# A decode attention and the output projection behind it as one phase, and a row norm moved into the MLP's first step

## The reference

```python
hn = rmsnorm(h, norm_attn[l])                   # h = x
q, k, v = split(hn @ w_qkv_a)                   # q, k rotated; 8 heads, 2 maps of 64
o = diff_attend(q, q_pos, k_all, v_all, k_pos, lam)   # softmax of map 0 - lam * softmax of map 1
o = rmsnorm(o, subln_a[i]) * (1.0 - lam_init)   # per head of 128 columns, lam_init = 0.2
h = h + o.reshape(b, t, A_V) @ w_o_a[i]         # the output projection, 1024 x 1024
h = h + sq_relu_mlp(rmsnorm(h, norm_mlp[l]), w_up[l], w_down[l])   # 1024 -> 4096 -> 1024
```

## Time and profile before

| | |
|---|---|
| median of 3 runs | 3811.17 us (3806.93 to 3812.57) |
| the profiled execution: its time, its span | 3813.02 us, 3811.3 us |
| TensorE busy | 3467.8 us (91%), mean granted clock 0.955 |
| VectorE, ScalarE, GpSimd busy | 1720.6, 1131.1 and 568.2 us (45%, 30%, 15%) |
| transfers | 325.21 MB, mean 85 GB/s |
| `fused_attention` | to 572 us |
| decode attention of layer A (`da`) | 572 to 809 us |
| output projection (`oa`) | 809 to 969 us |
| first MLP (`m0`) | from 969 us |

### The profile page before, as it was taken

How to read it: one execution, slowest core, us unless ns; L and a number is a source line. 1 busy time by engine, 2 the same in 40 slices (tenths; PEclk the granted TensorE clock), 3 DMA queues, 4 the chain that set the end, 5 groups by cost and what they waited for, 6 DMA issues and landing times. The chain is left out here.

```text
span 3811.3 us, 60654 instructions
## 1 busy us (share of the span) xinstructions
PE 3467.8 (91%) x23426; PEld 3048.8 (80%) x23426; DVE 1720.6 (45%) x2995; ACT 1131.1 (30%) x2287; POOL 568.2 (15%) x284
## 2 busy tenths in 40 slices
PE   6999997859799999998899888959969799999998
PEld 6999996748799999997787767746657699999997
DVE  4777764436344444445013266634423344444445
ACT  4444443433211122222013066633322222221112
POOL 3323200020111111110222000000010111111110
PEclk9999998979899999999799989979989899999999
DMA  3111119850211111110222243337751111111111
GB/s 112 54 54 53 46 27 349 330 172 28 72 33 44 44 44 44 38 39 2 82 90 72 62 95 82 67 90 264 276 202 38 61 44 41 36 44 44 44 44 50
DMA packets 263451, 325.21 MB, mean 85 GB/s; under 512 B 112945, under 2 KB 196049, under 8 KB 263313
## 3 DMA queue, kind: packets, MB, share of 16 engines
q1 hardware_dynamic: 248528, 288.85, 23.8%
q10 hardware_dynamic: 13648, 30.49, 2.2%
q0 software_dynamic: 1152, 4.19, 0.4%
HBM read 283.69 MB, written 39.79 MB: 85 GB/s over the span
## 5 line engine op out<-in xcount | busy, mean ns | idle before, releaser
L753 DVE TENSOR_TENSOR h_rows<-h_rows,m_dn 128x512 f32<-128x512 f32 x576 | 391.4, 686 | 325.4 <-PE m_dn L334 325.4
L332 PE MATMUL m_dn<-m_dn_hi,m_hid_hi 128*128 128x512 f32 x1152 | 449.4, 390 | 0.0
L333 PE MATMUL m_dn<-m_dn_lo,m_hid_hi 128*128 128x512 f32 x1152 | 448.4, 389 | 0.0
L334 PE MATMUL m_dn<-m_dn_hi,m_hid_lo 128*128 128x512 f32 x1152 | 448.2, 389 | 0.0
L737 DVE TENSOR_TENSOR m_relu<-m_relu 128x384 f32<-128x384 f32 x192 | 157.2, 819 | 516.6 <-ACT m_relu L718 516.6
L658 POOL TENSOR_TENSOR m_up_lo<-m_up_raw,m_up_hi 128x2048 fp32r<-128x2048 f32 x32 | 147.6, 4612 | 933.8 <-ACT m_up_hi L708 933.8
L332 PE MATMUL m_up<-c_xt_hi,m_up_hi 128*128 128x384 f32 x768 | 261.9, 341 | 16.6 <-POOL m_up_lo L658 16.6
L332 PE MATMUL m_up<-b_xt_hi,m_up_hi 128*128 128x384 f32 x768 | 261.9, 341 | 16.6 <-POOL m_up_lo L658 16.6
L334 PE MATMUL m_up<-c_xt_hi,m_up_lo 128*128 128x384 f32 x768 | 259.6, 338 | 0.0
L333 PE MATMUL m_up<-b_xt_lo,m_up_hi 128*128 128x384 f32 x768 | 259.6, 338 | 0.0
L333 PE MATMUL m_up<-c_xt_lo,m_up_hi 128*128 128x384 f32 x768 | 259.5, 338 | 0.0
(11 more groups left out here) (319 smaller groups left out, 7210.4 us busy)
## 6 DMA issues: line engine op xcount, KB each, us to landing
da_k_tiles<-in_cache_a_k SPq DMA_DIRECT2D x64, 512.0 KB, 5.9
da_v_tiles<-in_cache_a_v SPq DMA_DIRECT2D x64, 512.0 KB, 5.5
m_up_raw<-in_w_up SPq DMA_DIRECT2D x32, 1024.0 KB, 5.4
m_dn_raw<-in_w_down SPq DMA_DIRECT2D x32, 1024.0 KB, 4.9
db_k_tiles<-in_cache_b_k SPq DMA_DIRECT2D x64, 512.0 KB, 4.6
db_v_tiles<-in_cache_b_v SPq DMA_DIRECT2D x64, 512.0 KB, 4.2
fa_w_raw<-in_w_qkv_a SPq DMA_DIRECT2D x48, 256.0 KB, 3.6
kv_w_raw<-in_w_kvf SPq DMA_DIRECT2D x16, 512.0 KB, 3.7
```

The source lines that it names most:

```text
L332: pe.matmul(out, lh, rh, start=start, stop=False)
L333: pe.matmul(out, lh, rl, start=False, stop=False)
L334: return pe.matmul(out, ll, rh, start=False, stop=stop)
L753: dve.tensor_tensor(hc, hc, dns[n % 3][:], ALU.add).then_inc(s_de, 1)
```

## The change

- `start_phase` is gone. Its loads (identity, gain, the other constants, the lambda vectors) are issued from ACT's queue at the start of `fused_attention`, and lambda is worked out in turns 1 and 2 of its loop.
- In `fused_attention`, ACT scales the first two weight halves by the gain while rounding them, and DVE makes their low parts; GpSimd keeps the others. The sums of squares of rows 3 to 8 are spread over turns 1 to 3, and their root is taken in turn 4. After each output tile ACT also squares it and sums it (`output_squares`, 64 small instructions) into `o_rstd`.
- `decode_project` replaces `decode_attention` of layer A and `oa`. Its steps are numbered `n` over all streams (9 per stream). From step 14 on, prompt row tile `r` takes 9 steps: in the first (`t` = 5) its 8 transposes, in each of the other eight 6 matmuls of 128x512 of its projection. The loops over streams are unrolled. SP loads `w_o_a` (4 MB, in 8 parts) between key tiles 3 and 4 of the first stream; ACT and DVE split it in steps 0 to 7, with the gain and the 0.8 in it. GpSimd scales the row by `o_rstd` (`scale_rows`). SP loads a row and its residual per stream (`load_rows`), behind a wait for the transposes of the row before. The last row tile, which holds the streams' own output, is stored, loaded, squared, scaled, transposed and projected after everything else.
- There is one bank for the transposed probabilities where there were two.
- `mlp_phase` of layer A does the row norm of its input itself (`pre`, tiles `m_first_`, in the buffers of `m_next_`): rows 0 to 3 ahead of the weights on ACT and DVE, rows 4 to 8 after the up groups 0 to 3; TensorE transposes three rows ahead of each column group `g`.

```diff
+        PRE_ROWS, PRE_LAST = [[4, 5], [6], [7], [8], [], []], 3
...
-            def step(i, last=False):
-                pe.wait_ge(s_ul, i + 2)
+            def step(i, last=False, rows=False):
                 for g in range(RG):
+                    if rows:
+                        for r in range(3 * g, 3 * g + 3):
+                            pre.tensor(pe, r)
+                        pre.ready(pe, 3 * g + 2)
+                    if g == 0:
...
+                    if rows:
+                        for r in PRE_ROWS[n]:
+                            pre.scalar(act, r)
+                        if n == PRE_LAST:
+                            pre.high(act, RT - 1)
...
+            if pre:
+                for r in range(4):
+                    pre.scalar(act, r)
             up_high(0)
-            with act.Fori(0, STEPS - 1) as i:
+            if pre:
...
+            act.dma_start(core.const[:, 0:P], table[:, 0:P]).then_inc(s_id, 16)
+            act.dma_start(gcol[:], gain.rearrange("(k p) -> p k", p=P), allow_slow_non_contiguous=True).then_inc(s_gain, 16)
+            act.dma_start(core.const[:, P:], table[:, P:]).then_inc(s_cst, 16)
+            for x, v in enumerate(lams):
+                act.dma_start(lv[:, x, :], v.rearrange("a d -> (a d)").partition_broadcast(P)).then_inc(s_lam, 16)
             x_high(0)
+            act.wait_ge(s_gain, 16)
             for k in range(HK):
                 weight_high(0, k)
-            x_square(1)
+            x_square(0)
             x_high(1)
             for k in range(HK):
                 weight_high(1, k)
-            for i in range(SLOTS + 3):
...
+                if i == 4:
+                    row_root(1, 3, RT)
+                if i == 1:
+                    act.wait_ge(s_dot, 2)
+                    act.activation(ex[:], dots[:], ACT.Exp).then_inc(s_le, 1)
                 v_rows(i - 1)
                 if i + 2 < RT:
...
+            def output_squares(j):
+                s = step(j)
+                if s is None:
+                    return
+                p, t = place(j)
+                bank_read(act, units["o", j])
+                if s:
+                    act.wait_ge(s_oq, s)
+                act.activation(osq[:], ost[:, s % 2], ACT.Square,
+                               accum_out=core.o_rstd[:, t, p:p + 1]).then_inc(s_oq, 1)
...
+        STEPS, FIRST = CT + 1, 14
...
+        def columns_of(n):
+
+            r, x = divmod(n - FIRST, STEPS)
+            return r if n >= FIRST and x == 0 and r < RT - 1 else None
+
+        def products_of(n):
+
+            r, x = divmod(n - FIRST, STEPS)
+            return (r, x - 1) if n >= FIRST and x and r < RT - 1 else None
...
+            def load_rows(r):
+                if r:
+                    sp.wait_ge(s_kt, 2 * use["x", r - 1] + 2)
+                sp.dma_start(orow[:], o_rows[r * P:(r + 1) * P, :]).then_inc(s_or, 16)
+                sp.dma_start(core.h[:, r, :], rows_of(*residual, r)).then_inc(s_h[r], 16)
...
+            for k in range(KT):
+                sp.dma_start(wraw[:, k, :], w_o[k * P:(k + 1) * P, :]).then_inc(s_wd[k], 16)
+            sp.dma_start(vn[:], v_new).then_inc(s_vn, 16)
+            for t in range(KR, CT):
+                load_k(0, t)
+            load_rows(0)
+            for b in range(1, NB + 1):
+                for t in range(CT + 2):
+                    if b < NB and t < CT:
+                        load_k(b, t)
+                    if t >= 2:
+                        load_v(b - 1, t - 2)
+                    if b >= 2 and t == 1:
+                        store(b - 2)
+                    if t == 7 and b < RT - 1:
+                        load_rows(b)
+            store(NB - 1)
+            sp.wait_ge(s_st, 16 * NB)
+            load_rows(RT - 1)
+
...
+            def scale_rows(r):
+                pool.wait_ge(s_or, 16 * (r + 1))
+                pool.wait_ge(s_qb, 2 * min(r + 2, NB) + 1)
+                o = orow[:].rearrange("p (h e) -> p h e", e=P)
+                if r in (0, RT - 1):
+                    pool.wait_ge(s_rt, 2 if r else 1)
+                root = core.o_rstd[:, r, :] if r < RT - 1 else stat[:]
+                pool.tensor_tensor(o, o, root.unsqueeze(2).to_broadcast([P, KT, P]), ALU.mult).then_inc(s_os, 1)
...
+            def row_products(r, x):
+
+                c, k0 = divmod(2 * x, KT)
+                if x == 0:
+                    banks_free(use["x", r] + 1)
+                if k0 == 0 and 2 * r + c:
+                    pe.wait_ge(s_av, 2 * r + c)
+                for k in range(k0, k0 + 2):
+                    if r == 0 and c == 0:
+                        pe.wait_ge(s_wl, k + 1)
+                    w = [v[:, k, c * HALF:(c + 1) * HALF] for v in (whi, wlo)]
+                    ins = product(pe, acc[:], (xhi[:, k, :], xlo[:, k, :]), w, k == 0, k == KT - 1)
+                if k0 + 2 == KT:
+                    ins.then_inc(s_am, 1)
+
...
+            for n, t, bs, bv in stages():
+                if products_of(n) is not None:
+                    row_products(*products_of(n))
+                if bv is not None:
+                    for pair in PROBS[t]:
+                        probs(bv, pair)
+                if bs is not None and t + 1 < CT:
+                    keys(bs, t + 1)
+                if bs is not None and t == CT and bs + 1 < NB:
+                    keys(bs + 1, 0)
+                if columns_of(n) is not None:
+                    row_columns(columns_of(n))
+                if bs is not None:
+                    scores(bs, t)
+                if bv is not None:
+                    for v in VALUES[t]:
+                        values(bv, v)
...
+            row_columns(RT - 1)
+            for x in range(KT):
+                row_products(RT - 1, x)
...
-        decode_attention(nc, core, "da", False, q[SEQ:ROWS, :], kv["ak_s"], kv["av_s"], cak, cav, None, None, None, ao,
-                         residual=(xp, xs))
+        decode_project(nc, core, "da", q[SEQ:ROWS, :], kv["ak_s"], kv["av_s"], cak, cav, ao,
+                       a["w_o_a"].rearrange("n d e -> (n d) e"), a["subln_a"][0, :].rearrange("(p o) -> p o", o=1), (xp, xs))
         with ExitStack() as rows:
             core.normed_rows(rows, "b")
-            dense_phase(nc, core, "oa", "head", a["subln_a"][0, :], ao,
-                        [(a["w_o_a"].rearrange("n d e -> (n d) e"), c, "add", c) for c in (0, HALF)],
-                        following=a["norm_mlp"][0, :])
```

More of the change, by code:

```diff
@@ L133, in scope, with __init__ @@
     return sb, ps, sem
[L137 to L178, removed]
 class Norm:
-    def __init__(self, core, sb, ps, sem, tag, kind, gain, src=None, buffers=2):
+    def __init__(self, core, sb, ps, sem, tag, kind, gain, src=None, buffers=2, share=None):
         self.core, self.kind, self.gain_src, self.src = core, kind, gain, src
-        self.xn, self.buffers = sb(f"{tag}xn", [P, buffers, D]), buffers
+        self.xn, self.buffers = share.xn if share else sb(f"{tag}xn", [P, buffers, D]), buffers
         self.own_rows = kind in ("rms", "final")
@@ L204, in __init__ @@
         if kind != "final":
-            self.bank = [ps(f"{tag}nt{i}", [P, 4, P]) for i in range(2)]
+            self.bank = share.bank if share else [ps(f"{tag}nt{i}", [P, 4, P]) for i in range(2)]
         self.s_pre, self.s_root, self.s_gain, self.s_sq, self.s_rs, self.s_xn, self.s_tp, self.s_hi, self.s_lo = (
@@ L625, in mlp_phase @@
         nxt = Norm(core, sb, ps, sem, "next_", "final" if y_rows else "rms", following, y_rows)
+        pre = Norm(core, sb, ps, sem, "first_", "rms", first, share=nxt) if first is not None else None
         NF, RG = FC // P, 3
@@ L693, in step @@
                         nxt.tensor(pe, r - 2)
-            with pe.Fori(0, STEPS - 1) as i:
+            if pre:
+                step(0, rows=True)
+            with pe.Fori(1 if pre else 0, STEPS - 1) as i:
                 step(i)
@@ L748, in step @@
                     low(n)
+                    if rows:
+                        for r in PRE_ROWS[n]:
+                            pre.vector(dve, r)
+                        if n == PRE_LAST:
+                            pre.low(dve, RT - 1)
                 for n in range(ND):
@@ L755, in step @@
                         nxt.vector(dve, r - 1)
-            with dve.Fori(0, STEPS - 1) as i:
+            if pre:
+                for r in range(4):
+                    pre.vector(dve, r)
+                step(0, rows=True)
+            with dve.Fori(1 if pre else 0, STEPS - 1) as i:
                 step(i)
@@ L761, in _, with fused_attention @@
             nxt.low(dve, RT - 1)
-def fused_attention(nc, core, tag, x_rows, gain, w, k_out, v_out, q_sample, o_rows):
+def fused_attention(nc, core, tag, table, lams, x_rows, gain, w, k_out, v_out, q_sample, o_rows):
     with ExitStack() as ctx:
@@ L903, in _ @@
             pool.wait_ge(s_gain, 16)
-            for n in range(2 * PAIRS):
+            for n in range(2, 2 * PAIRS):
```

(19 more changed lines are left out.)

461 lines of the change are left out of this document (439 added, 22 removed).

## The result

The changed kernel takes 3830.75 us (median of 5 runs, 3826.79 to 3832.03), the kernel before 3811.17 us (5 runs beside it): ratio 1.0053, 95% interval 1.0039 to 1.0066. It is slower by 19.6 us, where 33 us less were forecast. The profiled execution took 3832.03 us.

A forecast was written before the change was run, and what follows sets the result against it. Decode needs transfers, projection needs TensorE, and they stand one behind the other. Head -20, merged phase -54, MLP +40.5 sum to -33.5 from 3813.0: 3779.5, less 1.9, 3778 us; own range 3760 to 3792, ends 3750 and 3803.

The forecast's parts named there:

- Steps 14 to 71, "with 37 us a stream": Merged decode and projection: 37 us a stream between bounds of 31 and 38.7, so 58 steps take 238 us.
- the prediction's own sign of being wrong: Merged streams: the prediction called itself wrong if a stream took under 34 or over 40 us.
- half of the gaps filled: Merged streams: half of the 0.37 us gaps per step counted as remaining in the 37 us a stream.
- The end of the phase: After the merged steps: value-only steps 21 us instead of 26, then the last row's chain, 31 us in the sum.
- The head, "-20": Program start: turn 2 of `fused_attention` at 27 us instead of 47.33, a gain of 20 us, bounds 13 and 23.
- The first stream, "+5": Steps 0 to 7, where ACT and DVE also split 4 MB of weights: 5 us more, bounds 0 to 8.
- The MLP's first step, "+40.5": Norm in the MLP: first product +9.6 us, two pauses +26.6, lower clock +4.3; bounds +31 to +47.
- Number 2: Merged streams: value tiles queue behind the rows, TensorE waits 10.3 us a stream, 3831 us; chance 8%.
- Number 3: No tellable change: value-tile wait of 6 to 8 us, or unfilled gaps with head -13 us; 3811 us; chance 10%.
- Number 1: Merged streams: the decode's gaps are not filled, a stream takes 40 us, 3797 us; chance 20%.
- Number 4: MLP's first step: norm of rows 4 to 8 hides, two pauses go, 31 us less, 3747 us; chance 7%.
- The range's high end: Whole kernel: 3803 us, for the decode's gaps left unfilled together with a poorer head.

The follow-up runs named there:

- e_store_late: Changed kernel with SyncE issuing the output store at loop position 6 of a stream, not 1: 3798.02 us, ratio 0.9963.
- e_both_late: Changed kernel with the store at loop position 6, not 1, and the projection rows' loads at 9, not 7: 3776.64 us, ratio 0.9912.
- e_norm_move: Kernel before, with only the MLP's row norm moved into the MLP's first step: 3830.97 us, ratio 1.0045.
- e_head_only: Kernel before, with only the changed kernel's program start: 3798.92 us, ratio 0.9960.

## Why the prediction was wrong

The sign was wrong, and one step made it so. Against the profiled execution, 3832.0 where the sum said 3779.5:

1. *Steps 14 to 71, "with 37 us a stream".* **This step failed.** It was 44.3 us a stream, over 40, the prediction's own sign of being wrong. The six streams between 611.02 and 877.75 took 266.7 us where the sum has 222: 44.7 more. The sum went through SyncE's queue for the rows and value tile 6, and priced that wait at 2 us, once a stream; it came once a stream, 2.1 us in the mean. It did not go through the queue for the store, which the change also puts there, ahead of key tile 2. That wait stood in the sum at nothing, and it was 3.7 us in the mean. Nor did it price the lower clock behind either wait. With these the store costs 5.2 us a stream (44.3 to 39.1), the rows 2.8 (44.3 to 41.5). The 37 was meant for the rows ahead of value tile 6 and a store that blocks nothing. That kernel is `e_store_late`, and it took 39.1: 2 us too low even so. With both moved a stream takes 36.1 us, where the sum without its 2 us for the value tile says 35. So its other parts (half of the gaps filled, no gap worse) hold to about 1 us; each by itself was not measured.
2. *The end of the phase.* Forecast 68 us from the transposes of row 6 (16 + 21 + 31, the first for the four steps up to step 71), measured 77.3; in `e_both_late` 71 (828.2 to 899.3). So 6 of the 9 us are the same queue, in the last stream. The sum's terms for the last row's store (2.5 us) and load (4) stood on no row; they landed in 1.9 and 3.3 us.
3. *The head, "-20".* Turn 2 began at 26.2 us (forecast 27), but turns 2 to 4 then took 7 us more than before, 5.1 of them in two waits for VectorE's `fa_qT`; a microsecond came back later. -14.9: within the bounds, mis-sized by 5.1. The sum stopped at turn 2, where the gain was largest. No run tells the table loads from the rest of the head.
4. *The first stream, "+5".* Right: the first row's transposes came at 611.0, where the sum puts them at 605 plus the 5.1 us of the head.
5. *The MLP's first step, "+40.5".* Measured 82.6 us to the first down addition against 44.5 before (969 to 1013.5), +38. First product 24 us after the start (24.5), a row 4.57 us (4.65), the first pause 12.9 (13.3).
6. *Nothing for what lies behind the first MLP step.* 5 us come back there, from 24.2 us late at its first down addition to 19.1 at the end. Some 3.5 of them lie in the MLP's later steps: the up weights are asked for every 49.51 us, before every 49.78. `e_norm_move` has 49.51 too and `e_head_only` 49.77, so it comes with the norm's move; why is open.

The errors are +5.1 (head), +44.7 and +9.3 (streams and end), +0.9 (first stream), -2.3 (MLP) and -5.1: 52.6 us, and 3779.5 + 52.6 = 3832.1.

The rivals. Number 2 named the time, 3831 us, and not the cause. It had value tile 6 behind the rows, landing in 14.4 us as a residual tile had in the earlier trace rows, and a wait of 10.3 us a stream. A value tile landed in a median of 6.3 us and the wait was 2.1: by itself (`e_store_late`, where the rows stay) that wait left the kernel 0.37% faster than before. That its time came out is luck. Number 3 (no change) took the same wait at 6 to 8 us, or number 1, and fell with them. Number 1 (gaps unfilled, 40 us) fell with the 36.1 us. Number 4 (the norm hides) fell with the pauses. The range's high end, 3803 us, had no case in which SyncE waits for anything but rows, and that is why it did not hold the time.

What the parts are worth, from the experiments, if they add up: the start -10 to -15 us, the norm's move +17 to +22, and so the merged decode and projection about -35 to -43 with both orders mended (`e_both_late` as a whole is 0.88% of 3811 us faster, 33.5 us by the ratio and 32.3 between the medians), and 54 us more than that as it was delivered. No run has the merging alone. With both orders mended the phase took 340 us in the trace (559.1 to 899.3), against 342 in the sum and 397.0 as delivered: the merging did what the sum had it do once SyncE's list let it.

## What to carry to other kernels

When a transfer is moved to another engine's queue, write down for that queue, in order, which semaphore each entry waits for and when it comes, as for an instruction: a store that waits for the end of a pipeline must not stand ahead of loads that feed its beginning, and one place in the list decided 5 us a stream here. In the trace this fault is a pair: the consumer waits for a transfer while the transfer share is far from full. A wait of TensorE cost more than its length here, since the work behind it ran at a lower clock, so price it with that. And follow a gain at the head of a pipeline until the pipeline is full, not to its first turn.

## What the runs showed that I had not expected

- The clock's part of a stall: 11.8 us on top of 29.1 us of idle time in five streams, with two waits a stream of 1.8 to 4.3 us each. The granted clock was 0.95 in those streams and 1.00 without the waits.
- Over the five streams of the changed kernel, with bursts of eight tiles within 4 us among them, a key tile of 512 KB landed in a median of 7.4 us and a value tile in 6.3; in those of `e_both_late`, where the issues are more spread out, in 6.7 and 5.4 us. The medians differ by under 1 us; what costs is the time in which nothing is issued.
- The residual tiles landed in 5.5 us and not in 14.4 as in the earlier trace rows, with the same size and source. In the earlier trace rows eight of them had been issued at the phase's start.
